# Recurrent head with z tiles, gated outputs and norm inverse in PSUM, shared final rows, x in two transfers and c spread by TensorE

## The reference, cut to what matters

```python
mod = c @ w_ada[l] + b_ada[l]
shift, scale, gate = jnp.split(mod, 3, axis=-1)
h = rms_norm(x, g_pre[l]) * (1.0 + scale[:, None, :]) + shift[:, None, :]
proj = h @ w_in[l]
...
# mLSTM mixer, h of one head is 528 x 512
h = num / jnp.maximum(jnp.abs(den), jnp.exp(-m_row))[..., None]
h = h * lax.rsqrt(jnp.mean(h * h, axis=-1, keepdims=True) + RMS_EPS)
h = h * head_norm_w
h = h * jax.nn.sigmoid(o) * jax.nn.silu(z)
return h @ w_out
...
h = _rmsnorm(h, final_norm_w)      # the last step, 512 tokens are returned
```

## Time and profile before

| what | value |
|---|---|
| median of 3 runs | 1550.52 us (1546.44 to 1550.55) |
| the profiled execution | 1549.52 us |
| its span in the profile | 1547.8 us |
| granted clock of TensorE, mean | 0.991 |
| TensorE busy | 1491.0 us |
| VectorE, ScalarE, GpSimd busy | 737.2, 529.0, 596.6 us |
| moved by DMA | 140.28 MB |

### The profile page before, as it was taken

How to read it: one execution, slowest core, us unless ns; L and a number is a source line. 1 busy time by engine, 2 the same in 40 slices (tenths; PEclk the granted TensorE clock), 3 DMA queues, 4 the chain that set the end, 5 groups by cost and what they waited for, 6 DMA issues and landing times.

```text
span 1547.8 us, 24784 instructions
## 1 busy us (share of the span) xinstructions
PE 1491.0 (96%) x9498; PEld 1341.3 (87%) x9498; DVE 737.2 (48%) x1553; ACT 529.0 (34%) x944; POOL 596.6 (39%) x481
## 2 busy tenths in 40 slices
PE   3999999999999999999999999999999999999996
PEld 2788888888877999999999999888798889879875
DVE  6635766667667732433423311433623633362374
ACT  5534344343434323223222222323413332241232
POOL 5563231321355154344343354233443343344331
PEclk9999999999999999999999999999999999999997
DMA  9331111111243132222222222222121132212111
GB/s 382 110 125 66 55 54 54 56 53 55 109 168 131 56 109 82 81 104 85 82 88 85 99 82 86 77 96 90 60 102 68 61 108 81 95 59 104 67 43 55
DMA packets 23635, 140.28 MB, mean 91 GB/s; under 512 B 3352, under 2 KB 3352, under 8 KB 7712
## 3 DMA queue, kind: packets, MB, share of 16 engines
q1 hardware_dynamic: 18320, 127.93, 23.0%
q10 hardware_dynamic: 5264, 11.64, 2.2%
HBM read 137.45 MB, written 2.11 MB: 90 GB/s over the span
## 4 chain that ended last, share of the span: by engine, by line
issue 41%; PE 30%; POOL 23%; DVE 4%; ACT 1%; DMA 1%; POOLq 0%; DVEq 0%; ACTq 0%
PE lin L387 24%; POOL w_lo L328 23%; PE aux L931 3%; PE aux L903 1%; DVE mix L1795 1%; DMA residual<-x_t 1%; DVE square_sum L413 1%; PE aux L449 1%; POOL residual L360 0%; PE aux L912 0%; DVE squares L1813 0%; PE aux L421 0%; DVE tmp L1734 0%; DVE residual L1850 0%; DVE v_T L1791 0%
## 5 line engine op out<-in xcount | busy, mean ns | idle before, releaser
L328 POOL TENSOR_TENSOR w_lo<-w_raw,w_hi 128x512 fp32r<-128x512 f32 x448 | 583.0, 1333 | 918.6 <-ACT w_hi L375 918.6
L387 PE MATMUL lin<-x_hi,w_hi 128*128 128x512 f32 (+2 forms) x2056 | 556.8, 325 | 16.5 <-DVE x_lo L1330 6.9
L387 PE MATMUL lin<-x_lo,w_hi 128*128 128x512 f32 (+2 forms) x2056 | 551.2, 323 | 0.0
L387 PE MATMUL lin<-x_hi,w_lo 128*128 128x512 f32 (+2 forms) x2056 | 548.2, 321 | 0.0
L387 PEld LDWEIGHTS lin<-x_hi,w_hi 128*128 128x128 f32 x2056 | 341.0, 189 | 48.4 <-issue 9.6
L387 PEld LDWEIGHTS lin<-x_hi,w_lo 128*128 128x128 f32 x2056 | 340.9, 189 | 29.9
L387 PEld LDWEIGHTS lin<-x_lo,w_hi 128*128 128x128 f32 x2056 | 341.0, 189 | 25.9
L375 ACT ACTIVATE w_hi<-w_raw 128x1024 fp32r<-128x1024 f32 x224 | 223.8, 1049 | 150.9 <-PE lin L387 145.5
L1047 ACT ACTIVATE prob<-prob,neg_max 128x31 f32<-128x31 f32 (+6 forms) x128 | 60.2, 471 | 132.3 <-DVE neg_max L1458 132.3
L1601 DVE TENSOR_TENSOR conv_in<-conv_c_gate,lin 128x272 f32<-128x272 f32 (+1 forms) x30 | 11.6, 427 | 191.2 <-PE lin L387 191.2
L387 PE MATMUL lin<-mix,w_hi 128*128 128x512 f32 x256 | 81.8, 401 | 2.5 <-DVE mix L1795 1.9
(11 more groups left out here) (327 smaller groups left out, 1892.5 us busy)
## 6 DMA issues: line engine op xcount, KB each, us to landing
w_raw<-wstream SPq DMA_DIRECT2D x112, 1024.0 KB, 4.7
ada_shift_scale<-w_ada SPq DMA_DIRECT2D x8, 1024.0 KB, 20.7
ada_gate<-w_ada_gate ACTq DMA_DIRECT2D x4, 1024.0 KB, 5.5
residual<-x_t SPq DMA_DIRECT2D x1, 2048.0 KB, 10.3
residual<-x_t ACTq DMA_DIRECT2D x1, 2048.0 KB, 8.4
out_t<-residual ACTq DMA_DIRECT2D x8, 256.0 KB, 2.1
neg_m<-row_store ACTq DMA_DIRECT2D x4, 256.0 KB, 3.2
e_m<-row_store ACTq DMA_DIRECT2D x4, 256.0 KB, 3.1
```

Source lines behind the costliest of these rows:

```text
L328: eng.tensor_tensor(wlo[h][:, cols], raw[h][:, cols], whi[h][:, cols].bitcast(F32), ALU.subtract).then_inc(s_lo, 1)
L387: ins = t.matmul(o, w[half][:, c0:c0 + P], x(k, t0, cnt), start=(n == 0), stop=(n == 3 * kts - 1))
```

## The change

Seven things are done, all in the schedule; the result is the same.

1. x comes in two transfers, 5 tiles and 3 tiles. c comes as one row (4 KB) and TensorE spreads it by matmuls with a row of ones. The first chunk is issued behind the first modulation transfer. A root of a constant is taken before the squares.
2. The squares of x go to eight separate places (banks and two SBUF buffers). The sum is taken in two parts, and its first six tiles are summed over partitions while the last two are added.
3. GpSimd takes over the low part of the modulated tiles 3 to 7 (`x_low`) from VectorE, and its list is laid out anew. TensorE's order of steps is laid out anew too.
4. In the recurrent layer the z tiles are copied to `aux[3]`, the gated outputs to `aux[0]` and `aux[1]` (all PSUM). The head norm is one matmul of ones with the sum (128x512), a root and a reciprocal of 128x512 in `aux[2]`.
5. `head_rows` and `head_decays` move into their own head: behind tile 3 on VectorE, behind the split of the head's third chunk on ScalarE.
6. At the end the sum is taken in two parts and spread twice. ScalarE scales the last two tiles by the norm weight, GpSimd multiplies them by `rstd`, SyncE's queue stores them, and VectorE does the first six from the bank.
7. A semaphore of the attention outputs is replaced by VectorE's own counter.

```diff
+X_FIRST, LOW_DVE = 5, 3
+N_LAST_POOL = 2
...
-            eng.dma_start(res[:, :, META:T2], x_t).then_inc(s_x, 16)
-            eng.dma_start(raw[0][:], wstream[0, :, :]).then_inc(raw_full[0], 16)
+            eng.dma_start(res[:, 0:X_FIRST, META:T2], x_t[:, 0:X_FIRST, :]).then_inc(s_x, 16)
+            eng.dma_start(res[:, X_FIRST:, META:T2], x_t[:, X_FIRST:, :]).then_inc(s_x_rest, 16)
             for k in range(N_ADA):
-                if k == 4:
-                    eng.dma_start(raw[1][:], wstream[1, :, :]).then_inc(raw_full[1], 16)
+                if k in (1, 4):
+                    h = k // 4
+                    eng.dma_start(raw[h][:], wstream[h, :, :]).then_inc(raw_full[h], 16)
...
+            for k in range(KD - N_LAST_POOL, KD):
+                eng.wait_ge(s_xhat, N_LAST_POOL + k + 1)
+                eng.dma_start(out_t[P * k:P * k + P, :], res[:, k, META:T2]).then_inc(s_out, 16)
...
+            def x_low(k):
+                eng.wait_ge(s_xhi, k + 1)
+                eng.wait_ge(s_xlo, k)
+                eng.tensor_tensor(xlo[:, k, 0:T1], tmp[:, k % 2, 0:T1], xhi[:, k, 0:T1].bitcast(F32), ALU.subtract).then_inc(s_xlo, 1)
+            low_parts(0, 0, pieces=[0])
             eng.wait_ge(s_rstd, 1)
-            for k in range(KD):
-                eng.tensor_tensor(res[:, k, META:T2], res[:, k, META:T2], rstd[:, 0:T1], ALU.mult).then_inc(s_xhat, 1)
-                if 2 <= k < 2 + PIECES:
-                    low_parts(1, 1, pieces=[k - 2])
+            for k in range(3):
+                x_hat(k)
+            low_parts(0, 0, pieces=[1])
+            x_hat(3)
+            low_parts(0, 0, pieces=[2])
+            x_hat(4)
+            low_parts(0, 0, pieces=[3])
+            x_hat(5)
+            x_low(3)
+            low_parts(1, 1, pieces=[0])
+            x_hat(6)
+            x_low(4)
+            low_parts(1, 1, pieces=[1])
+            x_hat(7)
+            x_low(5)
+            low_parts(1, 1, pieces=[2])
+            x_low(6)
+            low_parts(1, 1, pieces=[3])
+            x_low(7)
...
+            eng.wait_ge(s_rstd, 2)
+            for k in range(KD - N_LAST_POOL, KD):
+                eng.tensor_tensor(res[:, k, META:T2], res[:, k, META:T2], rstd[:, 0:T1], ALU.mult).then_inc(s_xhat, 1)
...
-        gbuf = [tmp[:, 1, 0:T1], sq[:, 0, 0:T1]]
+        gbuf = [aux[x][:] for x in range(2)]
...
-            norm_total_pe(eng, n0, TB1, KD)
+            eng.wait_ge(s_c, 16)
+            for b in range(2):
+                ins = eng.matmul(c_spread[:, 512 * b:512 * b + 512], ones[0:1, :], c_rows[0:1, 512 * b:512 * b + 512], start=True, stop=True)
+            ins.then_inc(s_mod, 1)
+            eng.wait_ge(n0.added, KD - 3)
+            total_columns(eng, ssum, TB1, lambda j: aux[2], last=False)
+            eng.wait_ge(n0.added, KD - 2)
+            total_columns(eng, sq[:, 0, :], TB1, lambda j: aux[2], first=False).then_inc(n0.total, 1)
             norm_spread_pe(eng, n0, TB1)
...
+                for c, k in ([(0, k) for k in range(4)] + [(1, 0), (0, 4), (1, 1), (1, 2), (0, 5), (1, 3), (1, 4), (0, 6), (1, 5)]
+                             + [(0, 7), (1, 6), (1, 7)]):
...
                 head_projections(ii, (12,))
-                norm_total_pe(eng, hn, TB1, 4, ii)
+                eng.wait_ge(hn.added, ii * 3 + 3)
+                eng.matmul(aux[2][:], ones[:], ssum[:, 0:T1], start=True, stop=True).then_inc(hn.total, 1)
                 head_projections(ii, (13,))
-                norm_spread_pe(eng, hn, TB1, ii)
                 head_projections(ii, (14, 15))
...
                     chunk_lands_and_splits(eng, START["mlstm"] + c + 1, ii, 10)
+                    if c == 1:
+                        head_decays(ii)
...
-                        norm_root_act(eng, hn, TB1, DV, ii)
+                        eng.wait_ge(hn.total, ii + 1)
+                        act(aux[2][:], aux[2][:], ACT.Sqrt, bias=eps[:], scale=1.0 / DV).then_inc(hn.root, 1)
...
-            head_decays(0)
...
-                for j in range(2, 6):
+                for j in range(2, 4):
+                    copy_out_ml(j)
+                head_rows(ii)
+                for j in range(4, 6):
                     copy_out_ml(j)
...
-                    own.up(stt(sq[:, 1, 0:T1], sq[:, 1, 0:T1], 1.0, tmp[:, 0, 0:T1], ALU.add, ALU.mult))
+                    own.up(stt(aux[3][:], sq[:, 1, 0:T1], 1.0, aux[3][:], ALU.add, ALU.mult))
...
-                norm_invert_dve(eng, hn, TB1, ii)
-                eng.wait_ge(hn.spread, ii + 1)
-                copy(rstd[:, 0:T1], aux[2][:]).then_inc(s_hn_out, 1)
-                eng.wait_ge(s_hn_out, ii + 2)
+                eng.wait_ge(hn.root, ii + 1)
+                own.up(eng.reciprocal(aux[2][:], aux[2][:]))
+                own.settle()
                 z_out(1)
-                stt(gbuf[0], v_T[:, 0, 0:T1], hcur[:, 0:1], rstd[:, 0:T1], ALU.mult, ALU.mult).then_inc(s_g, 1)
+                stt(gbuf[0], v_T[:, 0, 0:T1], hcur[:, 0:1], aux[2][:], ALU.mult, ALU.mult).then_inc(s_g, 1)
...
-            norm_rstd_dve(eng, own, n4, TB1)
-            for k in range(KD):
-                stt(res[:, k, META:T2], res[:, k, META:T2], norm_c[:, 2, k:k + 1], rstd[:, 0:T1],
+            eng.wait_ge(n4.spread, 2)
+            for k in range(KD - N_LAST_POOL):
+                stt(res[:, k, META:T2], res[:, k, META:T2], norm_c[:, 2, k:k + 1], aux[2][:],
```

132 lines of the change are left out of this document (72 added, 60 removed).

## The result

The changed kernel takes **1529.38 us** (median of 4 runs, 1528.78 to 1530.52) against 1549.08 (1546.44 to 1550.55) for the kernel before, run beside it: ratio 0.9876, 95% interval 0.9858 to 0.9893, so 1.2% faster and clear of the scatter. The forecast was 1535.4, and its range began at 1530.5: the sign was right, the size not, and the result lies 1.1 us outside the range. The forecast stood on a median of 1550.52 for before. So 1.4 of the 6.0 us between forecast and result belong to that base, and 4.6 to the change, whose move is 19.7 us where 15.1 were forecast. The profiled execution took 1529.89, with a span of 1528.2.

The account below looks back on a forecast made before the run. TensorE's work and waits were taken to bound the kernel. Gains 5.0 + 2.5 + 2.8 + 4.0 + 0.8 = 15.1 us off the profiled 1549.52 made 1534.4; with 1.0 added for the median, 1535.4 us, range 1530.5 to 1542.5.

Parts of the forecast that it names:

- What bounds the kernel: Whole kernel: only what TensorE does or waits for has a price; it is busy 1491.0 of 1547.8 us.
- Step 1: Beginning: earlier x and low parts moved to GpSimd, the new pacemaker, bring the first gate matmul 5.0 us forward.
- the earlier landing: Beginning: a smaller first x transfer and c no longer beside it let the squares start 3.3 us earlier.
- GpSimd holds up the beginning: Beginning: GpSimd's 20 instructions run at 1.67, the two chunks end 1.0 us later than now; 1541.4 us, chance 0.12.
- Step 2: Start of the recurrent layer: decays behind the first split remove TensorE's wait for low parts; 2.5 us, bounds 1.5 and 2.5.
- Step 3: Head norm: one full precision matmul replaces 16 small ones, 0.7 us in each of 4 heads; 2.8 us, bounds 0 and 3.2.
- Step 4: VectorE's chain in heads: inputs in banks shorten products beside GpSimd, TensorE's waits go or shrink; 4.0 us, bounds 0 and 4.5.
- Step 5: End: fewer VectorE scalings and a dropped copy outweigh a second round of sums and spreads; 0.8 us, bounds -0.3 and 2.6.

Follow-up runs that it names:

- banks_only: Kernel before with only the z tiles and gated outputs put in PSUM banks, head norm as it was: 1542.81 us, ratio 0.9965.
- tail_only: Kernel before with only the new end (total in two rounds, two spreads, scalings shared out): 1547.25 us, ratio 0.9996.
- warm_all: Changed kernel with the two last spreads in the other order and needless matmuls in TensorE's waits at three norms: 1527.65 us.
- the three named above: Before with rows and decays moved, 1543.57 us; before with banks and norm changed, 1539.1; changed kernel with a needless 128x256 reciprocal in the last head, 1530.98.
- the swap: Changed kernel with the two last spreads of the inverse at the end in the other order, VectorE's first: 1527.81 us, ratio 0.9872.

## Why the prediction was right and wrong

- **What bounds the kernel**: right. TensorE's work stayed, its pauses went.
- **Step 1, the beginning** (5.0): right in mechanism, 4.62 measured. GpSimd set the pace up to tile 4 and TensorE waited for nothing behind it; the low parts back on VectorE cost 0.58. Both parts of the earlier landing were off (1.2 for 1.9, 1.7 for 1.4), and in part they made up for each other. The rival "GpSimd holds up the beginning" fell: its instructions take 1.28, not 1.67. Missing was what becomes of the 4.62 at the next norm: 1.24 were given back there, because the spread ran at half clock in this execution.
- **Step 2, the start of the recurrent layer** (2.5, upper bound 2.5): this step failed. It took the wait's length for the most that could be gained and gave TensorE's clock no term. Released by other engines, the old wait ended about 30 us behind the spread whatever TensorE did before, and hid a stretch at half clock. Measured: 2.8 with that stretch in both kernels, 4.39 in the pair of profiles, where only before has it.
- **Step 3, the norm on TensorE** (0.7 a head, upper bound 0.8): mis-sized. A head gives 0.9; 3.6 in four heads for 2.8. I had taken 0.4 off for the overlap of the small matmuls; the two rounds cost 1.8, not 1.6.
- **Step 4, VectorE's chain** (4.0, upper bound 4.5): mechanism right and now shown product by product. Sizes: a wait of 0.69 gone gives 0.94 (133.65 to 132.71 in `banks_only`); the last head's wait shrank to 0.24, not 0.5; and 1.54 of its 4.92 is the stretch at half clock behind the old wait, which has no term in the sum. The Trainium skill's price for a PSUM source (VectorE: DVE Perf Modes, section on the TRN2 errata) isn't found here: products with an input in a bank take 0.73 and 0.74 next to 0.75 from SBUF. The Trainium skill (SBUF — State Buffer, section Who interferes with whom) also says that a VectorE instruction with two SBUF inputs contends with a GpSimd instruction that reads SBUF. The traces agree: next to GpSimd's low parts such a product takes 1.0 to 1.1 us more (1.67 and 1.78 for 0.69 and 0.73).
- **Step 5, the end** (0.8; the terms as written add up to 0.65): 1.38 in the pair of profiles, but at full clock about nothing, and `tail_only` is not to be told from before.

Summed: 15.1 forecast, 19.6 measured. Of the 4.5 between them about 1.3 are sizes, at an equal clock: 0.3 at the start of the recurrent layer, 2.1 in norm and waits of the heads, less 0.4 at the beginning and 0.8 at the end. The other 3.3 are stretches at half clock that fell differently in the two profiles: 1.6 at 989, 1.5 at 1511 and 1.4 at the end, less 1.24 at block 1. **So what failed is that the sum had no term for TensorE's clock behind the beginning, in step 2 above all, where the wait's length stood as the upper bound; the sizes of steps 3 and 4 come second.** The clock's part is partly luck: of the kernels with the new order four profiles have the stretch at the spread and four don't (one of these with needless matmuls in its waits), and of the seven kernels with the long wait in the last head two have one behind it.

The low end of the range came from bounds that were too low in three places: step 2's (4.4 for 2.5), step 3's (3.6 for 3.2) and step 4's, which left out both the wider spacing and the clock (5.3 and 1.5 for 4.5). And it was close: had the base been 1549.08, the forecast would have been 1534.0 and the range would have begun at 1529.1, below the 1529.38 measured. What differs between executions of one kernel (stretches at half clock, the pace told of below) moves a time by a few us, which is of the size by which the runs of before scatter: 6.3 us over 42 of them, 1546.04 to 1552.32.

## What to carry to other kernels

Before pricing a wait by its length, ask which engine sets its end and what the waiting engine did just ahead of it: a slow stretch ahead of the wait is hidden in it, and one behind it is part of its price. Compare the granted clock stage by stage before giving a difference of two profiles to an edit: 4.4 us at one stage were 2.8 of the edit and 1.6 of the clock, and only the profiles of the other kernels told them apart. Where VectorE works next to GpSimd, move one input of each product into a bank; it was worth 1.0 to 1.1 us a product here. Look at the granted clock at each pause, and ask what sets the pace behind it before paying for a better one: a full clock behind block 1's norm bought nothing while VectorE set the pace.

## What the runs showed of the hardware that I had not expected

- Granted clocks of 0.50 came in stretches of 3.4 to 14 us, at the same few places (block 1's norm in all profiles but that of `warm_all`, the recurrent layer's spread in nine of fourteen, 121 us in two), but not in every execution of the same wait.
- Between 550 and 980 us, with TensorE never idle and the granted clock at 1.00, the profiles of before and of the changed kernel both ran 0.5% slower than the other twelve kernels: 483.1 us from the first projection behind block 1's norm to the next layer's spread, for 480.7 to 481.0 in nine of them and 481.5 in the three named above. Their rows for the same 60 us:

```profile
680.00:740.00 60.00, 60.00 (x492) 60.00 (x492) 19.51 (x33) 15.42 (x24) 25.83 (x21) 1.00 0.29 102
```

  in the changed kernel, and with the swap:

```profile
680.00:740.00 60.00, 60.00 (x496) 60.00 (x495) 21.34 (x36) 15.53 (x25) 25.21 (x20) 1.00 0.30 104
```

  The rows show 492 and 496 matmuls in 60 us. The slower pace falls alike on both kernels of the comparison and so stands outside its difference; what it is stays open.
- The periods of the three heads of a profile agree within 0.03 us (0.09 in `tail_only`), which makes a start-to-start table by stage far sharper than the medians: 0.94 and 1.06 us a head could be told apart where the total times scatter by 2 to 7.
